# Attention scores of a hybrid decoder layer: plain float32 matmuls replaced by stacked float32r halves

## What is computed

```
q = pad_front(q.reshape(b, l, ATTN_HEADS, 2, ATTN_QK_DIM))
k = pad_front(k.reshape(b, l, ATTN_HEADS, 2, ATTN_QK_DIM))
...
s = jnp.einsum('bqhmd,bkhmd->bhmqk', qi, k).astype(jnp.float32) * scale
p = jax.nn.softmax(jnp.where(mask, s, MASK_VALUE), axis=-1)
a = p[:, :, 0] - lam * p[:, :, 1]
return jnp.einsum('bhqk,bkhe->bqhe', a.astype(v.dtype), v)
```

## Time and profile before

| what | us |
|---|---|
| median of the three runs | 1175.62 |
| span of the profiled execution, first to last instruction | 1170.8 |
| TensorE matmuls busy | 1107.4 (95% of the span) |
| VectorE busy | 618.7 (53%) |
| ScalarE busy | 371.0 (32%) |
| GpSimd busy | 293.1 (25%) |
| mean granted TensorE clock | 0.996 of full speed |

### The profile page before, as it was taken

One profiled execution on the slowest core, in us unless ns is written; L12 is line 12 of the kernel. 1 busy time (PEld: TensorE's weight loads), 2 busy tenths in 40 slices (PEclk: granted clock), 3 DMA queues, 4 the chain that ended last, 5 costly groups with the idle time before them and its releaser, 6 DMA issues.

```text
span 1170.8 us, 18755 instructions
## 1 busy us (share of the span) xinstructions
PE 1107.4 (95%) x6761; PEld 1007.4 (86%) x6761; DVE 618.7 (53%) x1269; ACT 371.0 (32%) x816; POOL 293.1 (25%) x255
## 2 busy tenths in 40 slices
PE   4999999999999999999999999999999998999997
PEld 3799888999998789999887899998888997888886
DVE  6344675556246756561477565615776546225324
ACT  5213332223233322232332222333332324333324
POOL 5312121233211212322112133321211332432433
PEclk9999999999999999999999999999999999999999
DMA  5111011310210113103101121031012222863423
GB/s 186 37 39 38 18 37 37 89 50 26 93 54 18 37 44 84 54 20 105 42 18 37 55 73 54 19 115 30 19 36 64 71 81 81 345 224 124 154 81 144
DMA packets 91875, 85.88 MB, mean 73 GB/s; under 512 B 4478, under 2 KB 78316, under 8 KB 91788
## 3 DMA queue, kind: packets, MB, share of 16 engines
q1 hardware_dynamic: 91788, 84.70, 22.9%
HBM read 72.03 MB, written 12.66 MB: 72 GB/s over the span
## 4 chain that ended last, share of the span: by engine, by line
PE 48%; issue 33%; POOL 7%; DVE 6%; DMA 2%; ACT 2%; SPq 1%; POOLq 0%; DVEq 0%; ACTq 0%
PE ps L1326 22%; PE ps L1333 15%; POOL w_lo L725 5%; PE ps L1486 3%; PE ps L1318 2%; POOL small L712 2%; DMA acum_b<-acum_scratch 2%; PE ps L1500 2%; PE ps L1435 1%; DVE lm_buf L1204 1%; PE ps L1502 1%; DVE work L1132 1%; PE ps L1506 1%; ACT w_hi L794 1%; PE ps L1455 1%
## 5 line engine op out<-in xcount | busy, mean ns | idle before, releaser
L1326 PE MATMUL ps<-u_hi,w_hi 128*128 128x348 f32 x1152 | 389.8, 338 | 8.2 <-ACT conv_u L848 4.3
L1326 PE MATMUL ps<-u_lo,w_hi 128*128 128x348 f32 x1152 | 371.4, 322 | 0.0
L1326 PE MATMUL ps<-u_hi,w_lo 128*128 128x348 f32 x1152 | 371.2, 322 | 0.0
L1326 PEld LDWEIGHTS ps<-u_hi,w_hi 128*128 128x128 f32 x1152 | 218.6, 190 | 15.7 <-issue 5.4
L1326 PEld LDWEIGHTS ps<-u_lo,w_hi 128*128 128x128 f32 x1152 | 218.1, 189 | 0.8
L1326 PEld LDWEIGHTS ps<-u_hi,w_lo 128*128 128x128 f32 x1152 | 217.6, 189 | 0.0
L725 POOL TENSOR_TENSOR w_lo<-w_raw,w_hi 128x1024 fp32r<-128x1024 f32 (+1 forms) x56 | 129.2, 2307 | 190.3 <-ACT w_hi L794 190.3
L712 POOL TENSOR_TENSOR small<-small,m_half 128x1 f32<-128x1 f32 (+1 forms) x81 | 54.5, 672 | 458.4 <-DVE small L1179 308.9
L1333 PE MATMUL ps<-w_hi,u_hi 128*128 128x512 f32 x256 | 99.8, 390 | 4.1 <-DVE u_lo L977 3.3
L1333 PE MATMUL ps<-w_hi,u_lo 128*128 128x512 f32 x256 | 101.6, 397 | 0.0
L1333 PE MATMUL ps<-w_lo,u_hi 128*128 128x512 f32 x256 | 101.4, 396 | 0.0
(11 more groups left out here) (198 smaller groups left out, 1661.1 us busy)
## 6 DMA issues: line engine op xcount, KB each, us to landing
w_raw<-in_w_in SPq DMA_DIRECT2D x56, 512.0 KB, 3.8
work<-y_scratch SPq DMA_DIRECT2D x32, 512.0 KB, 3.6
acum_b<-acum_scratch SPq DMA_DIRECT2D x32, 256.0 KB, 4.1
w_raw<-in_w_out SPq DMA_DIRECT2D x32, 256.0 KB, 4.2
work<-in_x SPq DMA_DIRECT2D x8, 512.0 KB, 3.7
y_scratch<-ys SPq DMA_DIRECT2D x8, 512.0 KB, 3.2
work<-in_x SPq DMA_DIRECT2D x4, 1024.0 KB, 8.7
out<-work SPq DMA_DIRECT2D x8, 512.0 KB, 2.7
```

Of the source, the lines that this page charges most:

```text
L1326: ins = eng.matmul(dst, w[:, k, 0:m], u[:, k, cols], start=(k == 0 and n == 0), stop=(k == KD - 1 and n == 2))
```

## The change

Q and K of a head are now kept as float32r halves, as the projections' operands are. For map m, k_st[m] holds the rounded keys in the map's own 64 rows and their rest in the other 64 rows. q_hi[m] holds the rounded queries twice, in both halves; q_lo[m] holds their rest in the map's own rows, and zeros in the others. One pass of q_hi over k_st gives hi·hi + hi·lo, one pass of q_lo gives lo·hi. The meta keys are no longer apart: keys 0 to 15 + 128(s+1) are one run, cut at 512, so the runs are 144, 272, 400, 528, 656, 784, 912 and 1040 columns long. Where a cut falls into the mask's columns (at s = 3 and s = 7), the mask is added in two matmuls. "turn" reads the weights at their new places.

```diff
-        q_map = [part(LP), part(LP)]
-        k_t = part(LP)
+        q_hi = [q_hl[:, 0, :], q_hl[:, 1, :]]
+        q_lo = [q_hl[:, 2, :], q_hl[:, 3, :]]
+        k_st = [k_hl[:, 0, :], k_hl[:, 1, :]]
...
 # ScalarE, step "piece"
-                            eng.mul(q_map[0][0:QK, cols], src[0:QK, :], QK ** -0.5)
-                            eng.mul(q_map[1][QK:P, cols], src[QK:P, :], QK ** -0.5).then_inc(bank_free[a % 2], 1)
+                            of, to = query_cols(tc)
+                            eng.mul(q_hi[0][0:QK, to], src[0:QK, of], QK ** -0.5)
+                            eng.mul(q_hi[1][QK:P, to], src[QK:P, of], QK ** -0.5).then_inc(qk_hi_ok, 1)
+                        elif t == TK:
+                            eng.wait_ge(s_done, it * 2 * QB + 1)
+                            eng.copy(k_st[0][0:QK, cols], src[0:QK, :])
+                            eng.copy(k_st[1][QK:P, cols], src[QK:P, :]).then_inc(qk_hi_ok, 1)
...
 # VectorE, step "piece"
-                        if t == TK:
-                            eng.wait_ge(piece_done, it * PPI + a + 2)
-                            eng.wait_ge(s_done, it * 2 * QB + 1)
-                            eng.tensor_copy(k_t[:, cols], src).then_inc(done, 1)
+                        if t == TQ:
+                            of, to = query_cols(tc)
+                            eng.wait_ge(qk_hi_ok, it * 2 * PIECES + tc + 1)
+                            eng.scalar_tensor_tensor(q_lo[0][lo, to], src[lo, of], QK ** -0.5, q_hi[0][lo, to].bitcast(F32), ALU.mult, ALU.subtract)
+                            eng.tensor_copy(q_hi[0][up, to], q_hi[0][lo, to].bitcast(F32))
+                            eng.scalar_tensor_tensor(q_lo[1][up, to], src[up, of], QK ** -0.5, q_hi[1][up, to].bitcast(F32), ALU.mult, ALU.subtract)
+                            eng.tensor_copy(q_hi[1][lo, to], q_hi[1][up, to].bitcast(F32)).then_inc(done, 1)
+                        elif t == TK:
+                            eng.wait_ge(qk_hi_ok, it * 2 * PIECES + PIECES + tc + 1)
+                            eng.tensor_tensor(k_st[0][up, cols], src[lo, :], k_st[0][lo, cols].bitcast(F32), ALU.subtract)
+                            eng.tensor_tensor(k_st[1][lo, cols], src[up, :], k_st[1][up, cols].bitcast(F32), ALU.subtract).then_inc(done, 1)
...
 # TensorE, step "scores"
-                        for at in range(0, (s + 1) * P, 512):
-                            w = min(512, (s + 1) * P - at)
-                            last = at + w == (s + 1) * P
-                            eng.matmul(s_ps[:, at:at + w], q, k_t[:, META + at:META + at + w], start=True, stop=not last)
-                            if last:
-                                eng.matmul(s_ps[:, s * P:(s + 1) * P], ident_b[:, :], mask_b[:, :], start=False, stop=True)
-                        eng.matmul(s_ps[:, (s + 1) * P:(s + 1) * P + META], q, k_t[:, 0:META], start=True, stop=True).then_inc(s_done, 1)
+                        diag, nk = META + s * P, META + (s + 1) * P
+                        for at in range(0, nk, 512):
+                            end = min(at + 512, nk)
+                            masked = end > diag
+                            eng.matmul(s_ps[:, at:end], q_hi[m][:, qs], k_st[m][:, at:end], start=True, stop=False)
+                            ins = eng.matmul(s_ps[:, at:end], q_lo[m][:, qs], k_st[m][:, at:end], start=False, stop=not masked)
+                            if masked:
+                                a0 = max(at, diag)
+                                ins = eng.matmul(s_ps[:, a0:end], ident_b[:, :], mask_b[:, a0 - diag:end - diag], start=False, stop=True)
+                        ins.then_inc(s_done, 1)
```

More of the change, by code:

```diff
@@ L306, in tiles_of, with query_cols @@
     return -(-(min((tc + 1) * PW, L) - META) // P) + 1
+def query_cols(tc):
+    lo, hi = max(tc * PW, META), min((tc + 1) * PW, L)
+    return slice(lo - tc * PW, hi - tc * PW), slice(lo - META, hi - META)
 def token_cols(c):
@@ L334, in build @@
         w_lo = sb("w_lo", [P, 2, KD, P], F32R)
-        work = sb("work", [P, 12528])
+        q_hl = sb("q_hl", [P, 4, T], F32R)
+        k_hl = sb("k_hl", [P, 2, LP], F32R)
+        work = sb("work", [P, 8348])
         taken = [0]
@@ L341, in part @@
             return work[:, taken[0] - n:taken[0]]
-        q_map = [part(LP), part(LP)]
-        k_t = part(LP)
+        q_hi = [q_hl[:, 0, :], q_hl[:, 1, :]]
+        q_lo = [q_hl[:, 2, :], q_hl[:, 3, :]]
+        k_st = [k_hl[:, 0, :], k_hl[:, 1, :]]
         v_t = part(LP)
-        gate = part(LP)
         prob_flat = part(2 * L)
@@ L357, in build @@
         raw = part(3 + LP)
-        y_raw = work[:, 0:OB * T].rearrange("p (b n) -> p b n", b=OB)
-        h_res = work[:, OB * T:OB * T + QB * D].rearrange("p (t d) -> p t d", t=QB)
-        assert OB * T <= 4 * LP and OB * T + QB * D <= taken[0] <= 12528
+        y_raw = q_hl[:, :, :].bitcast(F32)
+        h_res = work[:, 0:QB * D].rearrange("p (t d) -> p t d", t=QB)
+        assert OB == 4 and QB * D <= taken[0] <= 8348
         y_hi = u_hi[:, :, :].rearrange("p k n -> p (k n)")[:, 0:OB * T].rearrange("p (b n) -> p b n", b=OB)
@@ L369, in build @@
         th_piece = sb("th_piece", [P, 2, PW])
-        v_blk = sb("v_blk", [P, QB, P])
-        a_t = sb("a_t", [P, QB, P])
         conv_b_s = sb("conv_b_s", [P, LP])
+        v_blk = conv_b_s[:, 0:QB * P].rearrange("p (n k) -> p n k", n=QB)
         conv_u = sb("conv_u", [P, 2 + LP])
+        gate = conv_u[:, 2:2 + LP]
         conv_g = sb("conv_g", [P, LP])
+        a_t = conv_g[:, 0:QB * P].rearrange("p (n k) -> p n k", n=QB)
         conv_y = sb("conv_y", [P, T])
@@ L510, in build @@
         v_meta_ok = sem("v_meta_ok")
+        qk_hi_ok = sem("qk_hi_ok")
         s_done = sem("s_done")
@@ L734, in iteration @@
                         ca, cb = token_cols(a)
-                        src = (k_t, v_t)[a % 2][:, 0:KD * (cb - ca)].rearrange("p (k n) -> p k n", k=KD)
+                        src = (gate, v_t)[a % 2][:, 0:KD * (cb - ca)].rearrange("p (k n) -> p k n", k=KD)
                         eng.wait_ge(u_hi_ok, a + 1)
@@ L832, in iteration @@
                         src = pb[a % 2][:, 0:PW]
-                        if t not in (TK, TCH):
+                        if t != TCH:
                             eng.wait_ge(piece_done, it * PPI + a + 2)
@@ L847, in iteration @@
                             eng.wait_ge(convg_ok, it + 1)
+                            eng.wait_ge(attn_st, it * 16 + 32)
                             eng.copy(conv_u[:, 2 + tc * PW:2 + (tc + 1) * PW], src).then_inc(bank_free[a % 2], 1)
@@ L969, in _ @@
             own(eng, eng.memset(conv_u[:, 0:2], 0.0))
-            eng.memset(q_map[0][QK:P, :], 0.0)
-            own(eng, eng.memset(q_map[1][0:QK, :], 0.0))
+            eng.memset(q_lo[0][QK:P, :].bitcast(F32), 0.0)
+            own(eng, eng.memset(q_lo[1][0:QK, :].bitcast(F32), 0.0))
             eng.memset(dt_rows[:, META:P], 0.0)
@@ L1000, in iteration @@
                         n = cb - ca
-                        dst = (k_t, v_t)[a % 2][:, 0:KD * n].rearrange("p (k n) -> p k n", k=KD)
+                        dst = (gate, v_t)[a % 2][:, 0:KD * n].rearrange("p (k n) -> p k n", k=KD)
                         eng.wait_ge(x_tr, a + 1)
@@ L1103, in iteration @@
                         done = bank_free[a % 2]
-                        if t == TK:
-                            eng.wait_ge(piece_done, it * PPI + a + 2)
-                            eng.wait_ge(s_done, it * 2 * QB + 1)
-                            eng.tensor_copy(k_t[:, cols], src).then_inc(done, 1)
+                        lo, up = slice(0, QK), slice(QK, P)
+                        if t == TQ:
[9 more added lines that the diff above has]
+                            eng.tensor_tensor(k_st[1][lo, cols], src[up, :], k_st[1][up, cols].bitcast(F32), ALU.subtract).then_inc(done, 1)
                         elif t == TG:
@@ L1448, in iteration @@
                         for n in range(a + 1):
-                            turn(t_ps[n // 4][:, (n % 4) * P:(n % 4 + 1) * P], prob[0][:, n * P:(n + 1) * P])
-                        turn(o_ps[0:META, 0:P], prob[0][:, (a + 1) * P:(a + 1) * P + META]).then_inc(a_tr, 1)
+                            turn(t_ps[n // 4][:, (n % 4) * P:(n % 4 + 1) * P], prob[0][:, META + n * P:META + (n + 1) * P])
+                        turn(o_ps[0:META, 0:P], prob[0][:, 0:META]).then_inc(a_tr, 1)
                     elif step == "values":
```

3 lines of the change are left out of this document (1 added, 2 removed).

## The result

The changed kernel takes 1183.75 us (median of 4 runs, 1181.38 to 1186.86), the kernel before beside it 1175.01 (1174.05 to 1178.89). The ratio is 1.0089, 95% interval 1.0069 to 1.0109: slower by 0.9%, some 9 to 10 us. The forecast was 1173.0 and "about the same"; the time lies inside its range, near the upper end, but the direction is wrong.

The account below looks back on a forecast made before the run. TensorE's own list bounds the kernel, in flight for 95% of the span. Terms −35.7 + 12.2 + 6.6 + 2.2 + 3.6 + 8.5 = −2.6 take the profiled 1170.8 to 1168.2, or 1173.0 us as median; range 1157 to 1185.

Parts of the forecast that it names:

- the second rival: Clock: waits of about 1.8 us already bring falls, 12 falls costing 20.4 us instead of 8.5; 1185, chance 0.15.
- The scores, −35.7: Attention scores on TensorE: two float32r passes a run save 4.46 us a map, 35.7 us in the kernel.
- The rival with 144 columns at the plain price: Narrow score runs: 144-column passes cost 0.24 us, losing 3.4 us in all; 1176, chance 0.15.
- What VectorE takes back, 12.2: Attention, s = 4 to 6: attn_out stays behind the taps, so 3.06 us a head of saved scores is waited.
- Elsewhere I count nothing: Attention: no saved score time lost elsewhere; turns at s = 1, 2, 3 and 7 aren't among the twelve waits.
- Q2 and K1, 6.6 + 2.2: Ends of heads 0 to 2: VectorE's casts wait for GpSimd, Q2 2.2 us late each; K1 costs 2.2 in all.
- The first rival: Casts and clock mild: Q2 0.8 us late, K1 on time, no falls after new waits; 1158, chance 0.25.
- Head 0, 3.6: Before head 0: Q2's bank waits behind the chain on dt, K1 starts 5.7 us late; net cost 3.6 us.
- Three more steps are priced at nothing: Q0's steps in AHEAD (1.6 us if cover is gone), the conv_u wait and the memory moves cost nothing.
- The clock, 8.5: Clock falls of 1.7 us: behind turn at s = 6 in four heads, 6.8, and one in three behind Q2, 1.7.
- Q2's wait of 2.2 lies close to the limit: Ends of heads: Q2's 2.2 us wait may lower the clock; one fall in three is counted, 1.7 us.
- the prediction asked for some 20: Sign on TensorE: its waits for VectorE grow by some 20 us, otherwise the prediction is wrong.

Follow-up runs that it names:

- e6: Changed kernel with VectorE's row maximum of map 0 and attn_out ahead of the taps, s = 3 to 7: 1169.26 us, 0.9970 of the kernel before.
- e8: Changed kernel with one score pass a run instead of two (product with Q's low half left out): 1184.13 us, 1.0096 of the kernel before.
- e1: Changed kernel with Q's two casts on ScalarE instead of VectorE: 1166.93 us, 0.9945 of the kernel before.
- e2: Changed kernel with Q's two VectorE casts replaced by two tensor_scalar reading PSUM: 1176.09 us, 1.0025 of the kernel before.
- e3: Changed kernel with VectorE's steps for Q0 and Q2 moved in AHEAD's order: 1173.63 us, 1.0008 of the kernel before.
- e4_filled: Changed kernel with seven unread 512-column passes on TensorE before turn's wait at s = 6: 1180.89 us, 1.0068 of the kernel before.
- e5: Changed kernel with the edits of e1 and e3 together: 1159.72 us, 0.9895 of the kernel before.

## Why the prediction was wrong

The direction was wrong, and that the time fell into the range was luck: the range reached up to the second rival (1185), whose twelve falls of the clock didn't happen (there were nine). By its own steps:

- **The scores, −35.7: right.** Passes of 512 and 16 columns cost 0.23 and 0.11. From start to start the traces show 31.0 us saved (22.9, and 8.0 of listed waits for the norm). Of the missing 4.7, 3.8 stand in map 0's times at s = 2, 3 and 5 to 7, the places where the next step waits for the norm, and 0.9 in map 1's at s = 2, in front of "values". The rival with 144 columns at the plain price is refuted by s = 0, where the starts are 0.06 and 0.12 apart (timeline after):

```profile
95.00 0.23 PE L1462 MATMUL ps<-k_hl,q_hl 128*128 128x144 f32 x1
...
95.06 0.28 PE L1463 MATMUL ps<-k_hl,q_hl 128*128 128x144 f32 x1
...
95.18 0.23 PE L1466 MATMUL ps<-mask_b,ident_b 128*128 128x128 bf16 x1
```

- **What VectorE takes back, 12.2: right mechanism, too small.** That the row maximum and attn_out are late because of the taps is shown by e6. The growth of turn's waits (3.6 us), the new waits for the norm (8.0) and the 4.7 above are 16.3 us. The step that failed is "Elsewhere I count nothing": I looked only at the turns among the twelve waits, and not at the step between the scores and turn. attn_out's transposition follows map 0's scores at once and needs the norm, which the longer scores had covered. That is 4.1 us more than forecast. e8 shows that with these waits the score passes no longer set the pace.
- **Q2 and K1, 6.6 + 2.2: right.** 3 × 1.83 and 0.71 + 2.22 + 0.72 = 3.65, together 9.1. That what is held beside GpSimd is VectorE's cast with both ends in SBUF is shown by e1 and e2. The pair of ports as the reason is the page's, and page and trace agree: the Trainium skill (SBUF — State Buffer, "Who interferes with whom") says that cast and tensor_scalar can take the shared pair when their operands allow it and that a step with one input in SBUF outside those modes doesn't contend; here the cast from SBUF lasted 1.54 and 2.30 us, scalar_tensor_tensor and tensor_scalar from PSUM 0.50, and the norm, a tensor_scalar with both ends in SBUF, 2.38 instead of 0.35. The page names copies beside casts, so it covers the copy of the earlier trace rows too, which the prediction overlooked. The first rival, that casts don't wait, is refuted by the same rows.
- **Head 0, 3.6: the step that failed worst for its size.** Head 0 began 7.5 us late, 3.9 more than forecast. The price put on Q2 behind the chain on dt held (5.5 us of waiting for K1 against 5.7). But "Three more steps are priced at nothing: Q0's steps in AHEAD stand before the last token tile's" was wrong: VectorE sits still until Q0 has been projected, and only then makes the low half that dt_piece 1 needs. 3.5 us of waiting, and the chain on dt ends 3.9 later. I had priced the lost cover by the duration of the moved steps (1.6), not by when they can start. e3 gives back 9.5.
- **The clock, 8.5: about right in its sum, by luck, and wrong in its rule.** There are nine falls instead of two. The forecast had a fall behind turn at s = 6 in four heads and one in three behind Q2. There were three behind turn; each head's end had one, behind Q2's 1.83 in heads 0 and 2, behind K1's 2.22 in head 1; AHEAD got two more, and the one in head 3's scan went. At 1.7 each, the six less the one are 8.5 us. In AHEAD TensorE is busy for only 2.74 and 3.12 us of the three falls, so they cost about half of that, 2.9 us by this estimate, against 1.7 before. The step that failed is "Q2's wait of 2.2 lies close to the limit": a limit between 1.78 and 1.95 us had been read from a trace in which 1.61 us brought a fall. In the changed kernel, too, turn at s = 4 with 1.82 never brought a fall in this profile, and Q2 with 1.83 did. Length alone doesn't decide, and neither does the place, by the counts given under e4_filled; what does stays open.

TensorE's waits for VectorE grew by 3.6 + 14.7 + 8.0 + 3.5 − 1.95 = 27.9 us, where the prediction asked for some 20. Of the 11.4 us by which it missed, 4.1 are VectorE's part in the attention, 3.9 head 0, and 0.3 the waits for Q2's and K1's banks. The other 3.1 I can't assign to a step: 1.6 of them lie at the ends of heads, 1.0 in head 3's scan and the output, 0.5 in the attention. The experiments point to the same places. The prediction put 6.6 + 2.2 + 3.6 + 1.7 = 14.1 us on the copying out of Q and K and on head 0; repairing both in e5 gave back 22.7. How much of the change's 10 us is clock stays open as well: the mean granted clock is 0.982 to 0.985 in its four executions and 0.993 to 0.999 in those of the kernel before beside the experiments, but e4, which raised it, doesn't show the gain clear of its interval.
